# Down products of a mixture-of-experts layer with the activations as stationary operand

## The reference, cut to what matters

```python
def expert_block(args):
    xblk, e = args
    gu = xblk @ w_gu[e] + b_gu[e]
    x_glu = jnp.minimum(gu[:, :F], SWIGLU_LIMIT)
    x_lin = jnp.clip(gu[:, F:], -SWIGLU_LIMIT, SWIGLU_LIMIT)
    act = x_glu * jax.nn.sigmoid(SWIGLU_ALPHA * x_glu) * (x_lin + 1.0)
    return act @ w_down[e] + b_down[e]          # the down product
...
y = yb.reshape(P, D) * row_gate[:, None]
out = jax.ops.segment_sum(y, row_tok, num_segments=N + 1)[:N]
```

## Time and profile before

| | |
|---|---|
| median of 3 runs | 1308.76 us (1308.35 to 1309.82) |
| profiled execution, its time | 1308.46 us |
| its span, first to last instruction | 1306.7 us |
| busy: DVE, PE, ACT, POOL | 1141.0, 1103.0, 950.8, 180.7 us |
| DMA | 445.55 MB, mean 341 GB/s |

### The profile page before, as it was taken

One profiled execution on the slowest core, in us unless ns is written; L12 is line 12 of the kernel. 1 busy time (PEld: TensorE's weight loads), 2 busy tenths in 40 slices (PEclk: granted clock), 3 DMA queues, 4 the chain that ended last, 5 costly groups with the idle time before them and its releaser, 6 DMA issues.

```text
span 1306.7 us, 48498 instructions
## 1 busy us (share of the span) xinstructions
PE 1103.0 (84%) x21802; PEld 967.7 (74%) x21803; DVE 1141.0 (87%) x868; ACT 950.8 (73%) x881; POOL 180.7 (14%) x69
## 2 busy tenths in 40 slices
PE   5999998788888888888888888888888888888874
PEld 2455555788888888888888787887878888878873
DVE  5742544799999999999999999999999999999994
ACT  5232423578888888888888888888888888888873
POOL 0121200003333333200000020000200000100020
PEclk9999998899999999999999999999999999999987
DMA  9512221899999999999999999999999999999964
GB/s 348 209 43 87 95 115 65 316 361 379 404 405 405 405 405 406 405 405 402 398 401 399 398 397 403 402 397 394 403 403 398 399 402 396 402 401 396 397 251 142
DMA packets 87354, 445.55 MB, mean 341 GB/s; under 512 B 8897, under 2 KB 9409, under 8 KB 54273
## 3 DMA queue, kind: packets, MB, share of 16 engines
q1 hardware_dynamic: 82400, 427.99, 81.3%
q0 software_dynamic: 3472, 12.19, 4.8%
q10 hardware_dynamic: 1296, 2.44, 0.6%
HBM read 426.21 MB, written 16.38 MB: 339 GB/s over the span
## 4 chain that ended last, share of the span: by engine, by line
DVE 30%; DMA 28%; PE 18%; issue 17%; ACT 5%; DVEq 0%; SPq 0%; ACTq 0%
DVE ring L393 21%; DMA ring<-in_w_down_dram 14%; DMA ring<-in_w_gu_dram 9%; PE ps L1079 8%; PE ps L1181 4%; DMA arena<-in_w_gu_dram 4%; ACT ring L390 4%; PE ps L413 3%; DVE arena L468 2%; DVE arena L480 1%; DVE arena L483 1%; DVE arena L474 1%; DMA arena<-in_x_dram 1%; DVE arena L489 1%; PE ps L1117 1%
## 5 line engine op out<-in xcount | busy, mean ns | idle before, releaser
L413 PE MATMUL ps<-arena,ring 128*128 128x88 f16 x18432 | 783.2, 206 | 156.4 <-DVE ring L393 99.0
L413 PEld LDWEIGHTS ps<-arena,ring 128*128 128x128 f16 x18432 | 743.5, 100 | 188.2 <-DVE ring L393 96.4
L393 DVE SCALAR_TENSOR_TENSOR ring<-ring 128x2048 f16<-128x2048 f32 x290 | 655.3, 2285 | 23.2 <-ACT ring L390 22.0
L390 ACT ACTIVATE ring<-ring 128x2048 f16<-128x2048 f32 x290 | 549.9, 1907 | 111.8 <-DMA ring<-in_w_gu_dram 62.6
L463 POOL DMA_INDIRECT acc<-arena,slot_row x31 | 155.7, 5021 | 969.6 <-ACT arena L500 969.6
L393 DVE SCALAR_TENSOR_TENSOR ring<-arena,ring 128x2048 f16<-128x2048 f32 x94 | 212.9, 2285 | 5.6 <-ACT ring L390 4.8
L390 ACT ACTIVATE ring<-arena 128x2048 f16<-128x2048 f32 x94 | 178.9, 1907 | 27.2 <-DMA arena<-in_w_gu_dram 21.3
L406 PE MATMUL ps<-arena 128*128 128x88 f16 x2048 | 93.6, 207 | 6.6 <-DVE count_max_i L1594 3.3
L406 PEld LDWEIGHTS ps<-arena 128*128 128x128 f16 x2048 | 86.3, 101 | 7.6 <-issue 7.5
L1079 PE MATMUL ps<-ring,arena 128*128 128x512 f16 x384 | 87.5, 387 | 0.9 <-DVEq L1406 0.9
L1079 PEld LDWEIGHTS ps<-ring,arena 128*128 128x128 f16 x384 | 38.0, 99 | 45.2 <-issue 2.8
(11 more groups left out here) (136 smaller groups left out, 540.9 us busy)
## 6 DMA issues: line engine op xcount, KB each, us to landing
ring<-in_w_gu_dram SPq DMA_DIRECT2D x194, 1024.0 KB, 17.2
ring<-in_w_down_dram SPq DMA_DIRECT2D x96, 1024.0 KB, 15.5
arena<-in_w_gu_dram SPq DMA_DIRECT2D x62, 1024.0 KB
arena<-in_w_down_dram SPq DMA_DIRECT2D x32, 1024.0 KB
ring<-in_w_in_dram SPq DMA_DIRECT2D x4, 2048.0 KB, 12.6
ring<-in_w_out_dram SPq DMA_DIRECT2D x2, 2048.0 KB, 8.7
arena<-in_x_dram SPq DMA_DIRECT2D x4, 512.0 KB, 11.9
ring<-in_w_in_dram SPq DMA_DIRECT2D x2, 1024.0 KB, 11.2
```

The source lines that it names most:

```text
L390: return act.activation(split_of(slot)[:, 0, :], raw(r), ACT.Copy, scale=SCALE_W)
L393: return dve.scalar_tensor_tensor(split_of(slot)[:, 1, :], raw(r), SCALE_W, split_of(slot)[:, 0, :], ALU.mult, ALU.subtract)
L413: mm = pe.matmul(o, w[:, i, col:col + P], src[:, j, k, :], start=start and n == 0, stop=stop and n == 2, skip_group_check=True)
```

## The change

The down product takes the activations (128 x 88) as the stationary operand and 512 columns of weights as the moving one. Its result has tokens on partitions, in banks 4 and 5 (`ROWS`), and is copied by `act_row` from there. The copy `yT` and its scaling, the transposes and their semaphores go; the scale that `act_yT` applied goes into the gates (`act_slots`). `finish_rows` moves to where `turned_y` stood, ahead of chunk 4 of the stage, and waits for `chunk_used` itself. PE's wait for `row_ready` moves ahead of the gather that writes banks 4 and 5.

```diff
+        ROWS = ps[0:CAP, 4:6, :]
...
         def pe_down(pe, slot, f):
-            for d in range(KD):
-                mm = product(pe, YT[:, d // 4, (d % 4) * CAP:(d % 4 + 1) * CAP], split_of(slot),
-                             (f % 2) * D + d * P, actT, f, f == 0 and d % 4 == 0, f == KD - 1)
-            return mm
-
-        def pe_turn_rows(pe):
-            for d in range(KD):
-                mm = pe.transpose(MISC[0:CAP, d // 4, (d % 4) * P:(d % 4 + 1) * P], yT[:, d, :], ident)
+            w = split_of(slot)
+            for half in range(2):
+                col = (f % 2) * D + half * 512
+                for n, (i, j) in enumerate(((0, 0), (0, 1), (1, 0))):
+                    mm = pe.matmul(ROWS[:, half, :], actT[:, j, f, :], w[:, i, col:col + 512], start=f == 0 and n == 0,
+                                   stop=f == KD - 1 and n == 2, skip_group_check=True)
             return mm
...
-                           MISC[0:CAP, 1, 4 * CAP:4 * CAP + 2], ACT.Copy, accum_out=slot_gate[0:CAP, bass.ds(e, 1)])
+                           MISC[0:CAP, 1, 4 * CAP:4 * CAP + 2], ACT.Copy,
+                           scale=1.0 / (SCALE_A * SCALE_W * SCALE_G), accum_out=slot_gate[0:CAP, bass.ds(e, 1)])
...
-        def act_yT(act, half):
-            return act.activation(yT[:, 4 * half:4 * half + 4, :].rearrange("p k c -> p (k c)"),
-                                  YT[:, half, :], ACT.Copy, scale=1.0 / (SCALE_A * SCALE_W * SCALE_G))
-
         def act_row(act, half, rows, scale):
-            return act.activation(rows[0:CAP, half * 512:(half + 1) * 512], MISC[0:CAP, half, :], ACT.Copy, scale=scale)
+            return act.activation(rows[0:CAP, half * 512:(half + 1) * 512], ROWS[:, half, :], ACT.Copy, scale=scale)
...
-            def turned_y(done):
+            def finish_rows(e, done, first=False):
                 act.wait_ge(chunk_used, done)
-                for half in range(2):
-                    act_yT(act, half).then_inc(yT_ready, 1)
-
-            def finish_rows(e, first=False):
-                act.wait_ge(row_turned, e + 1)
                 act.wait_ge(meta_ready, e + 1)
...
                 high(h, q, 3)
-                turned_y(nth(s, 0))
+                finish_rows(s - 2, nth(s, 0), first)
                 high(h, q, 4)
...
-                finish_rows(s - 2, first)
                 high(h, q, 8)
...
-                turn_rows(s - 2)
                 gate_up(s, q, 4, 4)
+                pe.wait_ge(row_ready, 2 * s - 2)
                 if not last:
                     gather(s + 1, 1)
...
-                    pe.wait_ge(row_ready, 2 * s - 2)
...
-            pe.wait_ge(yT_ready, 2 * E - 2)
+            pe.wait_ge(row_ready, 2 * E - 2)
             pe.wait_ge(act_ready, E)
             down(E, 0, 0)
             down(E, 1, 1)
-            turn_rows(E - 2)
             down(E, 2, 2)
             down(E, 3, 3)
-            pe.wait_ge(row_ready, 2 * E - 2)
-            turn_rows(E - 1)
```

More of the change, by code:

```diff
@@ L130, in build_program @@
         sig = reg_d[:, 1024:1024 + KD * CAP].rearrange("p (b c) -> p b c", b=GB)
-        yT = reg_r[:, 1024:1024 + KD * CAP].rearrange("p (k c) -> p k c", k=KD)
         y_row = reg_p[:, 1024:2048]
@@ L308, in build_program @@
         act_ready = sem("act_ready")
-        yT_ready = sem("yT_ready")
-        row_turned = sem("row_turned")
         row_ready = sem("row_ready")
@@ L320, in build_program @@
         more = {k: sem(f"more_{k}") for k in ("high", "low", "used", "onehot", "gathered", "xT", "biased",
-                                              "glu", "lin", "prod", "sig", "act32", "ah", "act", "yT", "turned",
+                                              "glu", "lin", "prod", "sig", "act32", "ah", "act",
                                               "row", "stored", "meta_done", "meta", "pad")}
@@ L976, in _ @@
             high(E // 2, 0, 1)
-            turned_y(nth(E, 0))
+            finish_rows(E - 2, nth(E, 0))
             act_high_part(E - 1)
@@ L982, in _ @@
             act.activation(wgT, ps[:, 0, :], ACT.Copy).then_inc(wgT_ready, 1)
-            finish_rows(E - 2)
             act.wait_ge(pad_cleared, 2)
-            turned_y(CH * E)
-            act.wait_ge(row_turned, E)
+            act.wait_ge(chunk_used, CH * E)
             for half in range(2):
-                act_row(act, half, y_last, SCALE_G).then_inc(row_ready, 1)
+                act_row(act, half, y_last, 1.0 / (SCALE_A * SCALE_W)).then_inc(row_ready, 1)
             act.wait_ge(counts_ready, 1)
@@ L1016, in one @@
                 act.wait_ge(more["used"], CH * n)
-                for half in range(2):
-                    act_yT(act, half).then_inc(more["yT"], 1)
-                act.wait_ge(more["turned"], n)
                 act.wait_ge(more["meta"], n)
@@ L1030, in skip @@
                 act.sem_inc(more["row"], 1)
-                for k in ("xT", "yT"):
-                    act.sem_inc(more[k], 2)
+                act.sem_inc(more["xT"], 2)
             further_blocks(act, one, skip, last_added)
@@ L1236, in _ @@
             gather(0, 0)
-            def turn_rows(e):
-                pe.wait_ge(yT_ready, 2 * e + 2)
-                pe_turn_rows(pe).then_inc(row_turned, 1)
             def gate_up(s, q, k, c):
@@ L1349, in one @@
                     mm.then_inc(more["used"], 1)
-                pe.wait_ge(more["yT"], 2 * n)
-                pe.wait_ge(more["meta"], n)
-                pe_turn_rows(pe).then_inc(more["turned"], 1)
                 pe.wait_ge(more["stored"], 16 * n)
@@ L1358, in skip @@
                 pe.sem_inc(more["used"], CH)
-                pe.sem_inc(more["turned"], 1)
             further_blocks(pe, one, skip, last_added)
```

## The result

The changed kernel takes 1300.23 us (median of 5 runs, 1297.68 to 1302.55) against 1308.76 us before: a ratio of 0.9938, interval 0.9921 to 0.9954.

The account below looks back on a forecast made before the run. DMA was taken to bound the stages and a chain starting with PE's down products the end; 1308.46 less 2.2 (fetches) and 0.5 (tail) gave 1305.8, as median 1306.1, rounded 1306.0 us, range 1302.8 to 1309.2.

Parts of the forecast that it names:

- The bound: Whole kernel: DMA, full from 300 us on, sets the experts' time, about 950 us; the end from 1268 us is its own chain.
- PE's sum: PE in a stage: +1.6 us, from 27.9 to 29.5 of 31.7, with the lateness caught up at cost 0.
- the moved rows: ACT's earlier row copies in a stage: wait 1.0 us for the scatter, cost 0, or 0 to 1 us if it slips.
- ACT: ACT in a stage: two copies of 450 ns go, 0.80 us as a pair; ACT is not the bound.
- Rival C: Down products in the stages: exposed loads of 88 columns make PE's stage 35.6 us, 1393 us in all; chance 0.03.
- Instruction fetch: Full DMA engines in the stages: 23% fewer of PE's instructions to fetch gives back 2.2 us.
- The row: Sign on the profile page: the instruction queue falls to some 2.2 MB instead of 2.83.
- the second stretch: Sign in the later stages, 9 to 30 before at 32.67 us each: about 32.6 us a stage.
- The tail: End of the run, from 1268.42 us on: rows ready 0.2 us sooner, 0.5 us gained in all.
- L1369 ... 3.9 us after PE's last matmul: End, bias products: they start at 1285.1 after the branch, gaining 0.2 us, up to 1.5 if the sequencer runs ahead; 0.5 taken.
- rival B: End: bias products start when the rows are ready, 1282.4, gaining 2.9 us instead of 0.5: 1303.6 us; chance 0.10.
- the reload of the sum: End: expert 30's earlier rows bring its scatter and this reload earlier, worth 0 since the bias products come later than both.

Follow-up runs that it names:

- e6: Changed kernel with the first gate-up chunk of stages 2 to 31 loaded without its last 256 columns: 1292.21 us, ratio 0.9874.
- e7: Changed kernel with 12 more down products of 512 columns a stage, repeats whose results are discarded: 1303.71 us, ratio 0.9961.
- e1: Changed kernel with the last expert's down product, copy, turn back and rows in the old form: 1305.19 us, ratio 0.9970.
- e15: Changed kernel with each down product of 512 columns split into four of 128, same stationary activations: 1310.21 us, ratio 1.0015.
- e8: Changed kernel with 14 unread matmuls of 512 columns in PE's gap before the last down products: 1299.63 us, ratio 0.9929.
- e11: Changed kernel with 120 idle semaphore increments a stage on POOL alone: 1300.60 us, ratio 0.9935.
- e2: Kernel before the change, with only the last expert's down product in the new form: 1308.32 us, ratio 0.9998.
- e3: Changed kernel with POOL holding the scatters of experts 0 to 29 until ACT's high part of chunk 7: 1300.45 us, ratio 0.9932.
- e4: Changed kernel with two unused copies of 352 columns put back on ACT ahead of each expert's rows: 1303.10 us, ratio 0.9960.
- e10: Changed kernel with the 14 unread matmuls of e8, and the last down products ordered by half of the columns: 1299.76 us, ratio 0.9923.
- e13: Changed kernel with 96 idle semaphore increments a stage on PE among the down products: 1363.90 us, ratio 1.0416.
- e12: Changed kernel with 20 idle increments behind each weight issue on SP, inside its loop, none on POOL: 1346.54 us, ratio 1.0282.
- e9: Changed kernel with 20 idle increments behind each weight issue on SP, loop written out, and 100 a stage on POOL: 1317.26 us, ratio 1.0056.

## Why the prediction was wrong

**The bound.** Right: DMA in the stages, a chain on PE in the end (e6, e7, e1).

**PE's sum, the moved rows, ACT.** Right: 29.1 to 29.3 us of 31.7, hidden. The scatter came earlier and POOL was held longer, 16.2 us a time on average, half of them over 19.5, as forecast; it landed 29.5 us after its issue instead of 20.2, since it starts that much sooner, and ACT lost 3.0 us to it in the whole run. Rival C's exposed loads did not show: in e15 four products, each with its own load of 88 columns, took 12.52/192 us each, part of them at the low clock, so a load costs far less than the 0.12 us with which it is recorded; at full clock 48 products of 512 columns took 10.53 us (e8), as the sum had them. The Trainium skill (TensorE: Matmul & The Clock Gate, Weight-path perf modes) reserves the fast load for 128 columns; no exposed part of the slower one is seen here.

**Instruction fetch.** Right in kind as far as is shown, mis-sized: 2.2 us were forecast from q8's share of the DMA time, 4.0 came, of which the span shows 3.1, because stage 1 lost 0.9. The row was right (148 blocks became 115); the second stretch was forecast at 32.6 us a stage and came to 32.4. A block of PE's costs the stages 0.137 x 29 / 33 = 0.12 us, against 0.06 us by its share (9.5 us over 150 blocks). Why twice as much stays open; POOL's blocks of 8 KB cost nothing visible (e11). The Trainium skill (Runtime: NRT & Kernel Launch, Instruction fetch mechanics) calls the cost of a block mostly hidden. If the gain goes by the blocks, as e15 suggests, it isn't hidden for PE here, where DMA is full.

**The tail.** Here the prediction failed, by 4.7 us: 0.5 us were forecast, 5.2 came. The step "L1369 ... 3.9 us after PE's last matmul" was taken with 0.2 us for the earlier rows and 0.3 for a sequencer that runs ahead. It ran 3.1 us ahead, and 2.6 us went (L1369 started 1.3 us after PE's last matmul). The observation for it was made in rival B and given a tenth; even B's 1303.6 us was 3.4 too long. The step also has no term for what follows: the bias products before ran half at the low clock because of this very stop, which the earlier trace rows show as 5.39 us for 6 of the 16 passes; the stop's going brought 1.9 us more. I had looked for the clock only in the products ahead. These cost 1.7 us at the lower clock (12.21 against 10.53 in e8) where 2.4 were costed, which is why the rows came 0.7 us sooner and not 0.2. Last, the reload of the sum was called worth 0 "since L1369 is later than both", true before, but not once L1369 came sooner (e2). How much of the 5.2 us an execution gets hangs on its branch: with one of some 6 us it was 3.1 to 3.8 (e3, e4, e7).

## What to carry to other kernels

Fewer, longer matmuls can pay twice beside their own time. Here the stages, which go at DMA's pace, were shorter with fewer instructions on PE, most likely because fewer are fetched. And PE's sequencer gets ahead, so that a branch, or a stretch of new code, is passed while PE still works. When a stop of an engine goes, cost also the work behind it at the clock that it has without the stop. And ask what is next in line before calling another transfer hidden.

## What was not expected of the hardware

PE's branch of `further_blocks` takes 3.5 to 3.6 us in before, after, e1, e2, e8, e10, e11 and e13, but 3.8 in e12, 4.3 in e15, 4.7 in e9, 5.8 in e7, 6.0 in e3, 6.2 in e4 and 7.2 in e6; why is open. The changed kernel hides the shortest only, which may be why its 5 runs spread over 4.9 us and those of before over 3.1; this was not tested. A semaphore raised by an idle instruction costs POOL 82 ns, not the 17 recorded. Twenty such instructions behind each weight issue on SP, with 100 on POOL, cost 0.54 us a stage, though the trace shows SP still waiting for 450 us in all in front of its issues.
